# Taking the attention values of two heads in one step, on the two halves of TensorE

## The reference, cut to what matters

```python
o_c = jnp.einsum('bghqn,bngd->bqghd', p_c, vc)                       # compressed: 15 keys
o_s = jnp.einsum('bghqm,bgqmd->bqghd', softmax(s_s), v_sel)          # selected: with 256 tokens, all 4 blocks
o_w = jnp.einsum('bghqs,bsgd->bqghd', softmax(where(mask_w, s_w, NEG_INF_2)), vw)
return gb[..., 0, None] * o_c + gb[..., 1, None] * o_s + gb[..., 2, None] * o_w
```

## Time and profile before

| | before |
|---|---|
| median of 3 runs | 1806.57 us (1805.0 to 1807.66) |
| span of the profiled execution | 1806.0 us |
| outside the span, by the median | 0.57 us |
| TensorE busy (PE) | 1747.5 us, 97% of the span |
| VectorE, ScalarE, GpSimd busy | 1382.4, 912.2, 261.5 us |
| mean granted TensorE clock | 0.991 |

### The profile page before, as it was taken

How to read it: one execution, slowest core, us unless ns; L and a number is a source line. 1 busy time by engine, 2 the same in 40 slices (tenths; PEclk the granted TensorE clock), 3 DMA queues, 4 the chain that set the end, 5 groups by cost and what they waited for, 6 DMA issues and landing times. The chain is left out here.

```text
span 1806.0 us, 35803 instructions
## 1 busy us (share of the span) xinstructions
PE 1747.5 (97%) x14215; PEld 1709.8 (95%) x14215; DVE 1382.4 (77%) x1621; ACT 912.2 (51%) x1267; POOL 261.5 (14%) x423
## 2 busy tenths in 40 slices
PE   6999999999999999999999999899999998899999
PEld 5999999999999999989999998899999997699999
DVE  6767798687668877767967789769888898778555
ACT  3433377763335433456533366566444556655443
POOL 1411110011002011010110134411110121200000
PEclk9999999999999999999999999999999998999999
DMA  9988857459876888746697847335889492137450
GB/s 347 372 305 277 298 171 256 152 176 327 298 270 233 281 286 289 261 176 221 239 320 258 298 160 252 106 121 198 298 301 286 136 242 98 48 129 256 166 184 24
DMA packets 256071, 411.42 MB, mean 228 GB/s; under 512 B 17975, under 2 KB 200801, under 8 KB 255841
## 3 DMA queue, kind: packets, MB, share of 16 engines
q1 hardware_dynamic: 223032, 290.79, 49.2%
q0 software_dynamic: 32432, 119.04, 17.7%
q10 hardware_dynamic: 504, 0.18, 0.0%
HBM read 408.90 MB, written 2.63 MB: 228 GB/s over the span
## 5 line engine op out<-in xcount | busy, mean ns | idle before, releaser
L2678 DVE TENSOR_TENSOR lo<-raw,hi 128x2048 fp32r<-128x2048 f32 (+1 forms) x257 | 582.0, 2267 | 234.5 <-ACT hi L2512 234.0
L2512 ACT CAST hi<-raw 128x2048 fp32r<-128x2048 f32 (+1 forms) x266 | 498.4, 1876 | 387.2 <-PE dacc L2244 186.1
L2242 PE MATMUL up<-operand_hi,hi 128*128 128x256 f32 x1952 | 554.4, 284 | 3.6 <-DVE lo L2678 3.6
L2243 PE MATMUL up<-operand_lo,hi 128*128 128x256 f32 x1952 | 553.8, 284 | 0.0
L2244 PE MATMUL up<-operand_hi,lo 128*128 128x256 f32 x1952 | 553.6, 284 | 0.0
L2242 PEld LDWEIGHTS up<-operand_hi,hi 128*128 128x128 f32 x1952 | 375.9, 193 | 4.5 <-DVE lo L2678 4.4
L2243 PEld LDWEIGHTS up<-operand_lo,hi 128*128 128x128 f32 x1952 | 376.0, 193 | 0.0
L2244 PEld LDWEIGHTS up<-operand_hi,lo 128*128 128x128 f32 x1952 | 375.9, 193 | 0.0
L2242 PE MATMUL dacc<-act_hi,hi 128*128 128x256 f32 x1056 | 300.6, 285 | 3.4 <-DVE act_lo L2891 3.4
L2244 PE MATMUL dacc<-act_hi,lo 128*128 128x256 f32 x1056 | 299.8, 284 | 0.0
L2243 PE MATMUL dacc<-act_lo,hi 128*128 128x256 f32 x1056 | 299.2, 283 | 0.0
(11 more groups left out here) (432 smaller groups left out, 2784.4 us busy)
## 6 DMA issues: line engine op xcount, KB each, us to landing
ada<-in_ada_w_dram POOLq DMA_DIRECT2D x224, 512.0 KB, 6.0
raw<-in_ffn_wg_dram SPq DMA_DIRECT2D x88, 512.0 KB, 4.9
raw<-in_ffn_wu_dram SPq DMA_DIRECT2D x88, 512.0 KB, 5.3
raw<-in_ffn_wd_dram SPq DMA_DIRECT2D x88, 512.0 KB, 5.1
raw<-in_ffn_w_up_dram SPq DMA_DIRECT2D x88, 512.0 KB, 4.5
raw<-in_ffn_w_down_dram SPq DMA_DIRECT2D x46, 512.0 KB, 4.4
raw<-in_hg_w_in_dram SPq DMA_DIRECT2D x32, 512.0 KB, 6.0
raw<-in_attn_w_qkv_dram SPq DMA_DIRECT2D x24, 512.0 KB, 7.0
```

Source lines behind the costliest of these rows:

```text
L2242: pe.matmul(o, stat[0], mov[0], start=start, stop=False, skip_group_check=True)
L2243: pe.matmul(o, stat[0], mov[1], start=False, stop=False, skip_group_check=True)
L2512: last = act.copy(put(slab(hi, s, SPL)), take(slab(raw, s, RAW)))
L2678: last = dve.tensor_tensor(put(slab(lo, s, SPL)), take(slab(raw, s, RAW)), put(slab(hi, s, SPL)).bitcast(F32), ALU.subtract)
```

## The change

`values` is now called for a pair of heads. It is called in iterations n = 4, 6, ..., 18 for pair n/2 - 2, that is heads n-4 and n-3; odd iterations have no values. Inside, the products of the two heads take turns, the even head on weight columns that write rows 0 to 63, the odd head on those of rows 64 to 127. `n_pt` has four places, the new ones in space that weights and compressed probabilities held earlier. The semaphore of finished values counts pairs, and the waits on it are renumbered.

```diff
-        n_pt = [view(7424 + 768 * j, 8192 + 768 * j) for j in range(2)]
+        n_pt = [view(o, o + 768) for o in (7424, 8192, 10272, 11296)]
...
-            def values(n):
-                bb, f, p, _, _ = nsa_head(n)
-                pe.wait_ge(S["npt_done"], n + 2)
+            def values(bb):
+
+                _, _, p, _, _ = nsa_head(2 * bb)
+                pe.wait_ge(S["npt_done"], 2 * bb + 3)
                 both = bank(dacc, 2 + bb % 2)[:, 0:SEQ]
-                if f == 0:
-                    if bb >= 2:
-                        pe.wait_ge(S["no_done"], bb - 1)
...
-                o = both[64 * f:64 * f + 64, :]
+                if bb >= 2:
+                    pe.wait_ge(S["no_done"], bb - 1)
...
                 for br, v in enumerate((vs_sb, vw_sb)):
-                    pt = n_pt[n % 2][:, br * 3 * P:(br + 1) * 3 * P]
                     for j in range(2):
-                        c = j * SEQ + p * P + 64 * f
-                        last = pe.matmul(o[:, j * P:SEQ], v[:, c:c + 64], pt[:, j * SEQ:SEQ + j * P], start=False,
-                                         stop=(f == 1 and br == 1 and j == 1), skip_group_check=True)
+                        for f in range(2):
+                            pt = n_pt[(2 * bb + f) % 4][:, br * 3 * P:(br + 1) * 3 * P]
+                            c = j * SEQ + p * P + 64 * f
+                            last = pe.matmul(both[64 * f:64 * f + 64, j * P:SEQ], v[:, c:c + 64], pt[:, j * SEQ:SEQ + j * P],
+                                             start=False, stop=(br == 1 and j == 1), skip_group_check=True)
                 last.then_inc(S["npv_pe"], 1)
...
-                if n >= 3:
-                    values(n - 3)
+                if n >= 4 and n % 2 == 0:
+                    values(n // 2 - 2)
...
-                if n >= 2:
-                    act.wait_ge(S["npv_pe"], n - 1)
-                act.copy(n_pt[n % 2], dacc[:, 0:768]).then_inc(S["npt_done"], 1)
+                if n >= 4:
+                    act.wait_ge(S["npv_pe"], n // 2 - 1)
+                act.copy(n_pt[n % 4], dacc[:, 0:768]).then_inc(S["npt_done"], 1)
...
-                act.wait_ge(S["npv_pe"], n + 1)
+                act.wait_ge(S["npv_pe"], bb + 1)
```

More of the change, by code:

```diff
@@ L1669, in turn_probs @@
                 last.then_inc(S["npt_pe"], 1)
-            def values(n):
-                bb, f, p, _, _ = nsa_head(n)
-                pe.wait_ge(S["npt_done"], n + 2)
+            def values(bb):
+                _, _, p, _, _ = nsa_head(2 * bb)
+                pe.wait_ge(S["npt_done"], 2 * bb + 3)
                 both = bank(dacc, 2 + bb % 2)[:, 0:SEQ]
-                if f == 0:
-                    if bb >= 2:
-                        pe.wait_ge(S["no_done"], bb - 1)
-                    r = slice(64 * (bb % 2), 64 * (bb % 2) + 64)
-                    pe.matmul(both, vc_sb[r, p * P:(p + 1) * P], c_pt[r, bb // 2 * SEQ:(bb // 2 + 1) * SEQ], start=True,
-                              stop=False, skip_group_check=True)
-                o = both[64 * f:64 * f + 64, :]
+                if bb >= 2:
+                    pe.wait_ge(S["no_done"], bb - 1)
+                r = slice(64 * (bb % 2), 64 * (bb % 2) + 64)
+                pe.matmul(both, vc_sb[r, p * P:(p + 1) * P], c_pt[r, bb // 2 * SEQ:(bb // 2 + 1) * SEQ], start=True,
+                          stop=False, skip_group_check=True)
                 for br, v in enumerate((vs_sb, vw_sb)):
-                    pt = n_pt[n % 2][:, br * 3 * P:(br + 1) * 3 * P]
                     for j in range(2):
-                        c = j * SEQ + p * P + 64 * f
-                        last = pe.matmul(o[:, j * P:SEQ], v[:, c:c + 64], pt[:, j * SEQ:SEQ + j * P], start=False,
-                                         stop=(f == 1 and br == 1 and j == 1), skip_group_check=True)
+                        for f in range(2):
[3 more added lines that the diff above has]
+                                             start=False, stop=(br == 1 and j == 1), skip_group_check=True)
                 last.then_inc(S["npv_pe"], 1)
```

## The result

The change made the kernel slower. The median went from 1808.56 us (seven runs, 1805.0 to 1810.48) to 1815.26 us (seven runs, 1812.12 to 1822.52); the ratio is 1.0045, 95% interval 1.0027 to 1.0062, or about 8 us (the medians themselves are 6.7 us apart). The kernel before has seven runs here where the forecast had three, and its median is 2.0 us higher for it. The runs of the changed kernel also spread over 10 us, those before over 5.5. The profiled execution has a span of 1811.7 us, 5.7 more than before. The device time of a run is 1.6 to 1.8 us above its span in all later runs; the span of 1806.0 us before thus fits the run of 1807.66 us, and not the median of 1806.57 beside which it was set.

What follows compares the result with a forecast made beforehand. The prediction took a ring of waits, 7.76 us per two heads in the last mixer's loop, as the bound. Phase -0.31, loop end -0.78 and clock +2.4 gave +1.3 us on 1806.57: 1807.9 us, range 1803.5 to 1811.5.

Steps and rivals of the forecast that it cites:

- the term of +2.4 us for the clock: Pauses ahead of even heads' turnings in the last mixer's loop: two clock falls in six, 1.2 us each.
- the ring's phase: Last mixer's head loop: five rounds of 7.76 us from head 5's bias bring head 14's turning 0.31 us earlier.
- the end of the loop: From head 14's turning to the end of the last values: 7.75 us instead of 8.53, 0.78 less.
- Rival 2: TensorE's clock falls in most pauses, four or more of 1.75 us: +5.9 us, so 1812.5; chance 0.10.
- TensorE's half share of the ring: Turning, compressed product, values and scores in the last mixer's loop: 3.86 of 7.76 us, which a lower clock slows.
- The halves side by side: Values of two heads in turn on both array halves overlap: 1.47 us a pair, against 2.90 for two heads before.
- the rival of 2.18 us: A pair's 16 weight loads don't overlap products: 2.18 us, +3.9, 1810.5; chance 0.06, shared with no overlap at all.
- The ring of 7.76 us: Chain of waits through even iterations of the last mixer's loop, one round per two heads: 7.76 us, against 7.74 before.
- TensorE's saved 11.4 us: TensorE's work on values over eight pairs falls by 11.4 us, almost all becoming waiting that frees nothing.
- The clock in the loop: Sign to look for: a lower granted clock for TensorE somewhere between 1525 and 1580 us.
- the renumbered waits and four places: ScalarE's copies of heads and results in the loop: no cost, from -0.1 to +0.3 us.
- The rival of a shorter ring: Last mixer's ring shrinks to VectorE's 7.01 us, for instance by scores starting early: -4.8 us, 1801.7; chance 0.10.

Runs made afterwards that it cites:

- Both profiles: Profiles of the changed kernel, from its first measurement and from a repeat with no edit, against the kernel before: ratio 1.0045, then 1.0040.

## Why the prediction was wrong

**The size of the clock term failed, not the mechanism.** The step that failed is the term of +2.4 us for the clock, two falls in six pauses at 1.2 us each; beside it the forecast had -1.09 us for the ring's phase and the end of the loop, in sum +1.3. The term of -1.09 measured -1.36 us, in the loop with the pauses filled. The clock's term was too small by a factor of three to six: 7.9 us in one profile and 13.5 in the other. The median, 1815.26 us, is 7.4 above the forecast and 3.8 above the end of the range; 2.0 of the 7.4 us are the median before, which was 1806.57 with three runs and 1808.56 with seven, and not the change. Rival 2, most pauses with a fall, 1812.5, had a chance of 0.10 and was the case that came.

Two things made it too small:
- *How many.* I took two falls from two pauses of 2.43 and 2.57 us without one and one of 2.94 with one. Both profiles have five. In the first, the pause ahead of head 4 came out at 1.97 us, the next four at 2.56 to 2.58 and the last at 3.28, not all 2.3: among other things, the scores of an even head start 0.57 us after the odd head's turning does (1552.89 to 1553.46), where I reckoned a turning at 0.78. But longer pauses aren't the whole of it, since two of the five falls followed pauses under 2 us, one of them ahead of head 2, which I hadn't counted. Pauses of 2.43 and 2.57 that stand alone, beside full work, said little of a row of them in thin work. Whether it is the pauses themselves or the smaller share of work around them that lets the clock fall stays open; the dummies change both.
- *What one costs.* I took 1.2 us a fall; measured are 1.6 in the first profile and 2.7 in the second, whose falls are longer. For a fall of 7 us I had reckoned half speed times TensorE's half share of the ring, 0.25 us for each us at the lower clock (0.34 is what 1.2 us makes of one half as long). Measured are 0.38 and 0.40. The lower clock set in at or soon after the pause, when TensorE's part of the ring begins, and so it lay on that part for much of its time: in the round at 1538.59 all four TensorE pieces were slow.

**Point by point.** The halves side by side: predicted 1.47 us a pair (1.43 to 1.53), measured 1.45. The rule on row groups, the rival of 2.18 us from the Trainium skill ("TensorE: Matmul & The Clock Gate", Part 3), doesn't hold here: 16 weight loads of 0.136 us, 2.18 us in all, went by in the 1.45 us of the pair, with both halves on the same rows. The ring of 7.76 us: measured 7.75. No gain from TensorE's saved 11.4 us: right, and it is the heart of the case (its busy time fell by 6.5 us only, where some 10 were forecast; the stretches at 1.2 GHz take longer for the same work). The clock in the loop: its direction right. No cost of the renumbered waits and four places: the chain shows none. The rival of a shorter ring: it came only where the order was changed. The advice of the Trainium skill against idle gaps between bursts of matmuls ("TensorE: Matmul & The Clock Gate", "Why this matters for your kernels") agrees with the trace: with the gaps filled, the loop had no fall, and without, five, the first two of them after gaps of 1.95 and 1.97 us.

What I had not weighed is what the order offers: the pause that I foresaw (2.58 us as measured) has room for the values that stood on the ring behind it (0.63 + 1.45). With the values ahead of the turning the ring loses them, and needs no halves in turn for that.

What stays open is the spread of the order with the pair's values in the pause and no dummies (1803 to 1810 us): it fits falls in some runs, which the run with its pauses filled and the mean clocks of the runs support, but no profile of one of the longer runs shows it.

## What to carry to other kernels

Follow the ring before the busy share: in a loop of several engines, work saved on an engine pays only where the engine's part of the longest ring gets shorter, and gathering two iterations' work into one puts both on one ring. (Here a ring is a cycle of waits that comes back to the same engine one or more iterations later.) Look for work that waits for nothing new and sits behind the instruction that starts the next engine, and move it into the pause ahead of that instruction. When an edit opens a row of TensorE pauses of about 2 us or more in thin work, as here, price the lower clock on TensorE's whole part of the ring and for most rounds; a few dummy products in the pause are a quick test of it, and here they were a cure.

## What the runs showed of the hardware

- Float32 products of 64 columns on alternate halves of the array run fully side by side, with different moving data and both halves writing one PSUM bank: 16 records in 1.45 us against 8 in 1.44.
- TensorE ran part of such products side by side even when they weren't in turn: 2.15 us for a pair written one head after the other, between 1.45 in turn and 2.90 for two heads apart.
- The same program had its clock fall at different rounds in two profiles, for some 21 and for 34 us; its runs spread over 10 to 13 us, and over 4 to 5 where the pauses were filled whole.
- With eight dummy products, 1.95 us together, in each pause of 2.6 the clock stayed at 2.4 GHz through the profiled loop; with four it was at 1.2 GHz for 7 us, half of them on the first turning, ahead of the dummies.
